# Dots first, then the pick of the head two ahead, in every tick of the expert stage

## The reference, cut to what matters

```python
q = (xb @ w_pq).reshape(PEER_BLOCK, PEER_HEADS, 2, HALF_KEY)
s = jnp.einsum('thpd,pnd->thpn', q, sub_keys)
sv, si = lax.top_k(s, TOPK)                      # TOPK = 16
comb = sv[:, :, 0, :, None] + sv[:, :, 1, None, :]
tv, ti = lax.top_k(comb.reshape(..., 256), TOPK)
eidx = take_along_axis(cidx, ti)                 # which expert rows
g = softmax(tv)
a = gelu(einsum('td,thkd->thk', xb, exp_u[eidx]))
y = einsum('thk,thkd->td', g * a, exp_v[eidx])
```

## Time and profile before

| | |
|---|---|
| Median of 3 runs | 4174.43 us (4171.16 to 4183.52) |
| Profiled execution | 4171.84 us, of which the span of the profile 4170.1 us |
| Busy: TensorE, VectorE, GpSimd, ScalarE | 2558.1 (61%), 2384.7 (57%), 2204.4 (53%), 735.1 us (18%) |
| Mean granted TensorE clock | 0.77 |
| DMA over the span | 1389.59 MB, 333 GB/s; 1112.72 MB of it by GpSimd's queue |
| Expert dots on VectorE (L2485) | 1056, 1259.1 us busy |
| Picks: 16 small operations each (L2471) | 1056, 231.5 us busy |

### The profile page before, as it was taken

The page is one execution under the profiler, slowest core; times in us unless marked ns, Lnnn a source line. Parts: engine busy times, 40 slices in busy tenths (PEclk is TensorE's granted clock), DMA queues, the critical chain, the costliest instruction groups (busy, mean ns, idle before and its releaser), DMA issues. The chain is left out here.

```text
span 4170.1 us, 41353 instructions
## 1 busy us (share of the span) xinstructions
PE 2558.1 (61%) x12437; PEld 1307.4 (31%) x12437; DVE 2384.7 (57%) x7787; ACT 735.1 (18%) x1304; POOL 2204.4 (53%) x2289
## 2 busy tenths in 40 slices
PE   5996989889968856558753434343343353334366
PEld 5994646547545422124420111010010010011012
DVE  3113555623589757766566676666667666766401
ACT  3104526421111111111121111111011011111001
POOL 2222010013245666666656776767767767767673
PEclk9998989889989978878975666666565665565588
DMA  4228697674499999999999999999999999999995
GB/s 137 56 82 243 207 321 240 221 263 140 164 375 331 378 394 365 407 403 407 396 395 408 395 395 383 409 394 409 408 388 409 409 391 397 407 393 396 392 405 216
DMA packets 521867, 1389.59 MB, mean 333 GB/s; under 512 B 54512, under 2 KB 167465, under 8 KB 521639
## 3 DMA queue, kind: packets, MB, share of 16 engines
q0 software_dynamic: 308000, 1112.72, 68.0%
q1 hardware_dynamic: 205198, 265.98, 19.9%
q10 hardware_dynamic: 8448, 8.26, 0.6%
HBM read 1351.31 MB, written 35.85 MB: 333 GB/s over the span
## 5 line engine op out<-in xcount | busy, mean ns | idle before, releaser
L2485 DVE CUSTOM_DVE_ANT_0 exp_U<-exp_ps_x,exp_U 128x1024 f32<-128x1024 f32 x1056 | 1259.1, 1222 | 743.0 <-DMA exp_U<-in_exp_u,exp_idx 742.8
L2130 PE MATMUL exp_ps_y<-exp_V,exp_spread 128*32 128x512 f32 x3968 | 787.6, 936 | 1313.1 <-DMA exp_V<-in_exp_v,exp_idxT 1312.4
L1938 POOL DMA_INDIRECT exp_U<-in_exp_u,exp_idx x1056 | 1002.7, 949 | 540.0 <-DVE exp_dots L2485 277.9
L1961 POOL DMA_INDIRECT exp_V<-in_exp_v,exp_idxT x992 | 943.3, 951 | 449.9 <-issue 263.3
L2130 PEld LDWEIGHTS exp_ps_y<-exp_V,exp_spread 128*32 128x32 f32 x3968 | 155.5, 145 | 1869.2 <-issue 1868.3
L2471 DVE SCALAR_TENSOR_TENSOR exp_picked<-exp_iota,exp_tif,exp_cidx 128x70 f32<-128x70 f32 x1056 | 231.5, 290 | 2.3
L1351 POOL CAST first_w_high<-first_gate_w 128x1024 fp32r<-128x1024 f32 x16 | 17.0, 1065 | 328.3 <-DMA first_gate_w<-in_w_in 278.3
L433 PE MATMUL inproj_ps_b<-inproj_x_high,inproj_w_high 128*128 128x352 f32 x480 | 156.5, 326 | 18.6 <-POOL inproj_w_low L414 18.6
L1046 ACT ACTIVATE att_kT<-att_ps_x 128x512 f32<-128x512 f32 x256 | 139.8, 599 | 123.2 <-PE att_ps_x L883 123.2
L883 PE MATMUL att_ps_x<-all_ident,heads_pages 128*128 128x128 f32 x1024 | 141.1, 282 | 27.1 <-PEq L115 13.5
L849 POOL DMA_DIRECT2D att_logits<-decay_rows x32 | 22.9, 716 | 253.1 <-ACT att_kT L1074 234.8
(11 more groups left out here) (331 smaller groups left out, 3984.9 us busy)
## 6 DMA issues: line engine op xcount, KB each, us to landing
heads_pages<-in_cache_k SPq DMA_DIRECT2D x256, 256.0 KB, 3.7
heads_pages<-in_cache_v SPq DMA_DIRECT2D x256, 256.0 KB, 4.5
exp_U<-in_exp_u,exp_idx POOLq DMA_INDIRECT x1056, 9.1
exp_V<-in_exp_v,exp_idxT POOLq DMA_INDIRECT x992, 9.2
inproj_w<-in_w_in SPq DMA_DIRECT2D x20, 512.0 KB, 4.8
first_gate_w<-in_w_in SPq DMA_DIRECT2D x16, 512.0 KB, 5.6
mix_query_w<-in_w_pq SPq DMA_DIRECT2D x8, 1024.0 KB, 8.7
exp_late_w<-in_w_in SPq DMA_DIRECT2D x16, 512.0 KB, 6.7
```

The lines of the kernel that those rows point to most:

```text
L1938: pool.indirect_dma_start(U[:, r % NU, :], None, io["exp_u"][0], bass.IndirectOffsetOnAxis(idx[:, tile_of(n) % 2, h * TOPK + k:h * TOPK + ...
L1961: pool.indirect_dma_start(ring[:, at, :], None, io["exp_v"][0], bass.IndirectOffsetOnAxis(idxT[:, t % 2, token:token + 1], 0))\
L2130: x = pe.matmul(yb[f][g * NS:(g + 1) * NS, :], spread4[:, g, m, :], ring[:, at, f * 512:(f + 1) * 512], start=m == 0, stop=final, skip_gro ...
L2485: dve.tensor_tensor_reduce(out=row, in0=xb[:, :], in1=row, scale=1.0, scalar=0.0, op0=ALU.mult, op1=ALU.add, accum_out=dots[:, n % 2, k:k ...
```

## The change

In a tick, `dot(n)` now comes before `pick(n + 2)`; until now the pick came first. Since picks read their scores later, the load of a score slot alone no longer proves that ScalarE has stored the last scores of the first tiles out of the memory under `mB`; so `late_weigh(0)` waits for the stores of heads 6 and 7.

```diff
--- before.py
+++ after.py
@@ -2493,6 +2493,9 @@
                 made(dve, "proj", x)
                 b = bank_of[("proj", x)]
                 m = mB[:, i, late_cols(c)]
+                if x == 0:
+                    for h in (PH - 2, PH - 1):
+                        dve.wait_ge(*first_stored(h))
                 if x >= 4 and r:
                     dve.wait_ge(e["late_mixed"], x // 2 - 1)
                 dve.tensor_tensor(tmpB[x // 2 % 2] if r else m, bank[b][:, 0:CB], sgB[:, x % 2, :], ALU.mult).then_inc(bank_free[b], 1)
@@ -2599,8 +2602,6 @@
             for n in range(LEAD):
                 pick(n)
             for n in range(LAST + 1):
-                if n + LEAD < NUNIT:
-                    pick(n + LEAD)
                 if 1 <= n <= NUNIT:
                     weights(n - 1)
                 for t in range(NT + 1):
@@ -2619,6 +2620,8 @@
                         finish(t)
                 if n < NUNIT:
                     dot(n)
+                if n + LEAD < NUNIT:
+                    pick(n + LEAD)
```

## The result

The change takes **18.8 us** off: the ratio to the kernel before is 0.9955, with a 95% interval of 0.9945 to 0.9965, over eight runs of each. The forecast was 4155.

What follows compares the result with a forecast made beforehand. VectorE was taken to set the pace early, then the bytes at about 400 GB/s plus stretches of empty DMA. Terms -9.0 - 9.0 - 2.5 + 1.5 = -19.0 us gave 4155 us from a 4174.4 median, range 4147 to 4170.

Steps and rivals of the forecast that it cites:

- The frame: Expert stage: VectorE sets the pace in ticks 3 to 7; later, with full queues at 400 GB/s, the bytes do.
- the mark: Sign against the prediction: the full stage, where DMA queues are full, moving less than 400 GB/s.
- Term 1: Start of the expert stage: the first dots begin 9.0 us sooner, without unit 2's pick ahead; -9.0 us, bounds -5 and -13.
- Term 3: At 1480 to 1490 us: unit 12's pick no longer waits 4.14 us for scores; -2.5 us, bounds 0 and -3.2.
- the small hole: DMA at 273 GB/s from 1480 to 1490 us, 3.2 us lost, laid to unit 12's pick waiting for scores.
- Term 2: Near 1570 us: unit 14's pick no longer waits 30.66 us for scores; -9.0 us, bounds 0 and -10.5.
- the hole: DMA at 31 GB/s from 1570 to 1580 us, 10.5 us lost in all including refilling.
- Term 4: ScalarE comes later; in tick 26 the weights of unit 26 wait about 7.3 us; +1.5 us, bounds 0 and +3.
- The cover in hand: In plain ticks GELU ends 7.0 us after the dots, its covering pick after 9.0: 2 us in hand.
- Only one large term: Rival: only the early first dots or the score wait pays, about -10 us, 4165; chance 0.20.
- ScalarE starves TensorE: Rival: in ticks 3 to 10 late ScalarE delays TensorE's mixing banks, +30 us, 4204; chance 0.08.
- Nothing changes: Rival: start and hole are made good elsewhere, say by an earlier full DMA; 4174, chance 0.07.

Runs made afterwards that it cites:

- e5: The changed kernel with ScalarE copying a tile of zeros ten times in each of ticks 3 to 7; 4167.73 us against 4154.72 for the changed kernel beside it.
- e3: The kernel before with only unit 14's scores loaded ahead of the late output weights on SyncE's queue; ratio 0.9975 to the kernel before.
- e11: The new order in tick 0 alone, then the order of the kernel before; ratio 0.9981 to the kernel before.
- e9: The changed kernel itself timed and profiled once more; ratio 0.9955 to the kernel before, 4154.72 us.
- e1: The changed kernel switched back to the old order behind the dots of unit 11; ratio 0.9968 to the kernel before.
- e2: The kernel before up to the dots of unit 8, the new order from those of unit 9; ratio 0.9977 to the kernel before.
- e4: The changed kernel with ScalarE's gates of the next head moved a tick later, behind GELU and two evictions; ratio 0.9941 to the kernel before.
- e12: The changed kernel with ScalarE's gates of the next head moved behind GELU, timed a second time; ratio 0.9952 to the kernel before.
- e10: The kernel before with only the added wait for the stores of heads 6 and 7, order unchanged; ratio 0.9998 to the kernel before.
- e7: The changed kernel with the first part of the mixing's late weights loaded one tick later; ratio 0.9949 to the kernel before.

## Why the prediction was right, step by step

**What bounds the kernel.** The frame held: VectorE sets the pace to tick 8, the bytes from there. e5 shows the first half (16.2 us of waits, 13.0 us of time), e3 the second (a filled hole of 10.5 us by the forecast's count, 10.4 us of time). The forecast called itself wrong if the full stage moved less than 400 GB/s. It moved 399 in the one profile of the change and 400 in the other; D15 to the last dot takes 2226.9 us before, and 2228.7 and 2227.5 in the change, and 1.5 to 1.9 us of W26 are in that. So the mark was drawn too close to the value itself, and the stage was not slower than that.

**Term 1, forecast -9.0.** D9 begins 9.9 and 12.8 us earlier in the two profiles of the change. The forecast had D3 about 9 us earlier, and it was 12.8 and 13.9. The place was right and the size a little low: besides the 9.0 us of P2, D0's own 2.4 us of waiting for rows went (it now runs 18.4 us without a bracket). D1's waits stayed, 6.8 us against 7.0, and there e11 gains 4.4 of its 6.8 us. Some 2 to 3 us come back in ticks 3 and 4: from 12.8 us earlier at D3 to 9.9 at D5 (13.9 to 12.0 in e9). What takes them wasn't tried. In the change D0 comes early and VectorE has a pick less to do before D1, both at once. e11 has only the early D0 and gains 7.1 us at D9, so most of this term comes without the pick left out.

**Term 3, forecast -2.5.** From D9 to D11, past P12 and the small hole, the change gains 3.9 us more (D11 13.8 earlier, D9 9.9), e9 1.7 (14.5 and 12.8) and e1 1.9 (13.7 and 11.8). The small hole is filled in all three (406 GB/s and more). No run takes this term by itself: e2 fills the same hole, and there D11 is only 3.5 us earlier where D9 was 5.9. So its size is argued from the windows and not shown.

**Term 2, forecast -9.0.** From D11 to D15 the change gains 7.7 us (21.5 less 13.8), 8.1 in e9. That the wait of P14 makes the hole is shown by e3, which removes the wait by another road. That a switch back brings it again is shown by e1, but only in part: e1 still gains 2.9 us in these ticks. The chain that I gave for what is late next, TensorE behind the output weights, then the V slots, was right too: GpSimd waits 13.29 us there for `weigh`. It is over at 1548.97, earlier than I said, as the weights too are asked for earlier (1512.09 against 1531.39, 16 us counted from pick 0).

The single runs don't simply add. Behind D11 e3 gains 10.2 us, nearly the whole hole, and the change 7.7 and 8.1. In the change there are two weak windows that e3 doesn't have:

```profile
1630.00:1640.00 10.00, 10.00 (x34) 3.94 (x35) 9.69 (x60) 3.38 (x6) 7.68 (x8) 0.95 0.95 332
1690.00:1700.00 10.00, 8.89 (x33) 2.20 (x32) 9.82 (x17) 0.00 (x0) 7.61 (x8) 1.00 0.95 323
```
```profile
1600.00:1700.00 100.00, 71.92 (x263) 26.76 (x256) 67.61 (x225) 13.04 (x21) 65.05 (x67) 0.86 1.02 408
```

The first fence is the change, the second e3. By the 410 GB/s of a full queue the first window costs 1.9 us and the second 2.1, but D15 begins at 1687.6, so only the first can be among the 2.5 us. In e9 they are weaker (356 and 388). VectorE is busy for 9.7 and 9.8 of 10 us in the two; what puts its work there in the new order wasn't tried. A further part of the overlap is the 2.9 us that e1 has of the same hole.

**Term 4, forecast +1.5.** W26 waits 7.39 us (forecast 7.3), and the cost up to D28 is 1.5 us by e4 and e12, 1.9 against the kernel before. It isn't settled to better than some 2 us: the windows of 10 us from 2250 on lack 3.9 us of traffic in the change and 3.0 in e9, and from D26 to D34 the change takes 356.4 and 354.1 us, e4, e12 and the kernel before 354.4 each. The cover in hand is 2.1 us at W6, as forecast (1.1 at W7). The table load takes 1.28 us and GELU starts 0.01 us behind it (1326.57 and 1327.86); the drain of 1.38 us that the Trainium skill (ScalarE: Activation LUTs, What ACT_TABLE_LOAD costs) adds does not show here, and the row decides. Nor do the waits of some 2 us in nine ticks come that the forecast worked out from it. Nine W that did not wait before have a second table load ahead of their GELU (25, 31, 35, 40, 41, 47, 49, 55 and 57). Of these only W31 waits, 1.8 us, and there five copies stand between as well.

**The rivals.** *Only one large term:* D12 does not stop at the late rows. It waits 24.9 us for gathered rows on the way, as I had argued, and so comes to the late sum at 1565.96, without a bracket, when TensorE has made both halves of the product (the second ran from 1548.64 to 1555.77). *ScalarE starves TensorE:* refuted, and by e5 more than by the change. With ScalarE 5.29 us later still, it is VectorE's W that waits, and TensorE's brackets go on naming VectorE. The mechanism that a later ScalarE would have had is therefore another than I gave: for 5.3 us of added work a tick, 2 us are in hand and about 3 are paid. *Nothing changes:* refuted by e3 and e11 one by one.

**The sum.** -19.0 was forecast and 18.8 measured (20.5 by the medians). That is nearer than the terms deserve, and luck in part. Up to the last dot the change gains 19.7 and 22.0 us, more than the 19.0 of the forecast in both, and behind it the close takes 236.1 and 233.3 us against 231.0 (231.2 in e10). Nothing of the kind was in my sum. Kernels with the old order in the late ticks closed in 232.4 (e3), 233.7 (e1) and 234.1 us (e11), so it isn't shown to belong to the change; it stays open.

## What to carry to other kernels

Order on an in-order engine is worth what the first consumer behind it waits for: ask of each operation moved back not how long it takes, but which wait it uncovers or covers, since here a pick hides GELU (2.1 us in hand at W6), the landing of rows (6.8 us in e11), or nothing. Cut a kernel first into the stretch that an engine paces and the stretch that the bytes pace; in the one a lost microsecond stays lost (e5), in the other only an empty DMA counts (e3). And a wait caused by a load behind other loads can be removed on either side: one moved load gave 10.4 us without any reordering of VectorE (e3).

## What the runs showed of the hardware that was not expected

**A small VectorE operation held up by GpSimd.** Changed kernel, VectorE and then GpSimd:

```profile
1262.39 0.18 DVE L2442 CAST exp_sif<-exp_si 128x32 f32<-128x32 uint32 x1
1262.60 1.44 DVE L2443 TENSOR_SCALAR exp_sbase<-exp_sif 128x16 f32<-128x16 f32 x1
```
```profile
1263.10 0.90 POOL L1946 TENSOR_TENSOR exp_late_m<-exp_late_m,mix_attT 128x336 f32<-128x336 f32 x1
```

The same TENSOR_SCALAR takes 0.17 us in tick 3 (at 1231.21). Here it takes 1.44 and ends at 1264.04, as GpSimd's addition does (1264.00). It is so once more in this profile (1.55 us at 1322.54), and in the kernel before: 1.55 us at 1335.60 beside an addition at 1336.20. Of GpSimd's sixteen additions in the changed kernel only these two lengthen an operation by more than 0.2 us; those that meet a dot, a MAX8 or an index find leave its length as it is. The Trainium skill (SBUF — State Buffer, SBUF: two separate sides) describes an exclusive lock on the port pair that the two engines share; the trace agrees in that the two end together, with 1.3 and 1.4 us lost. It does not agree plainly with what is said there, that whichever starts first holds the ports, since VectorE's operation is recorded as starting 0.5 us ahead of the addition; GpSimd's spans in a profile are rough. No run here removed the addition, so the cause is argued and not shown.

**When a load lands is not when it is asked for.** With the DMA at 371 GB/s from 1187 to 1232 us, e7 began to ask 19.0 us later and had its last piece out 10.9 us later, and the use moved by 1.9 us. The issues themselves take SyncE's time: four pieces took 24.3 us in the changed kernel, 16.1 in e7.

**Where two profiles of one kernel differ.** The start of the expert stage moved by up to 9.4 us between the profiles, with the same code ahead of it. Distances from a fixed instruction agreed to 3 us, in one pair to 3.8, and so told more than single spans.
